# A mixing stage with its phase table from sine and cosine, GpSimd begun sooner, weight splits put ahead of head norms, and the operator products behind the gate

## The chip, the cores and the metric

The kernel runs on one core of one Trainium2 chip. The metric is the device time of one execution in microseconds (us). The profile describes one execution, whose own time stands beside it in the table below.

## The reference

Two blocks follow each other on a sequence of 256 tokens with 1024 channels, all in float32. The first block has two layers, and each layer has a mixing stage and a feed-forward stage:

```
proj = rms_norm(h) @ w_in
u_ssm, u_g, v_g, q, k, v = split(proj)
y_ssm  = s5_mixer(u_ssm, ...)
y_sgu  = spatial_gating(u_g, v_g, ...)
y_diff = diff_attention(q, k, v, ...)
h = h + concat([y_ssm, y_sgu, y_diff]) @ w_out
h = h + conv_gated_mlp(rms_norm(h))
```

The S5 mixer is a diagonal complex recurrence: `a_bar = exp(lam * dt)`, `states[n] = a_bar * states[n-1] + b_bar @ u[n]`, `y = real(c @ states) + d * u`, followed by a GELU and a gate. The differential attention normalises the query and key heads, rotates them, and takes the difference of two softmaxes. The second block is one layer with three attention branches; the change does not touch it.

## The kernel before

Each engine has a block of its own (`@block.sync` for SP, `@block.tensor`, ACT's, GpSimd's, which the profile calls POOL, and VectorE's), in which its instructions stand in the order in which they are issued. Semaphores join the engines. Nothing is scheduled by a planner: the written order is the order.

**Weights.** All weights stream in pairs of 512 KB in the order of `STREAM`. SP loads pair p into one of 7 slots (`LOADS`) of `raw`. ScalarE copies it, rounded, to `whi` (`hi_upto`, L1057; 6 slots, `HIGHS`). VectorE writes the rest, `raw - whi`, to `wlo` (`lo_upto`, L1612). TensorE then adds three products for each pair (L546 to L548 where a token tile is taken alone, L583 to L585 for 256 wide chunks, L590 to L592 otherwise). Once a pair is used, `pair_used` frees its slots. `hi_upto(n)` and `lo_upto(n)` are called at chosen places of the two engines' orders; this sets which split stands ahead of which other work. In layer 0 pairs 0 to 3 are the queries, 4 to 7 the keys, 8 and 9 the S5 input (`ssm_u`), 10 to 13 the gMLP, 14 to 17 the values, 18 to 25 the output projection.

**The mixing stage.** The chunks go through two pairs of PSUM banks in turn (`A` and `B` in the code), and `emptied` makes a chunk wait until the previous user of its banks has been read (`EMPTIED`: for the keys' bank, the rotary products `k_terms` and the squares `hsq_ready`). For queries and keys ScalarE squares the heads (`head_squares`), VectorE sums them (`head_sums`, L1738), GpSimd takes the inverse roots (`head_powers`), VectorE rotates (`rotary`, L1727 to L1732). The gMLP waits for the keys' bank.

**The S5 part** works in chunks of 4 tokens. From the decay parameters (L1669 to L1688, small VectorE operations) GpSimd makes powers of `a_bar` (`amplitude_powers`), multiplies them into the input matrix (`input_powers`, L409 to L412) and the output matrix (`output_powers`, L397 to L399). TensorE projects the inputs (`input_products`, L682); VectorE turns them by a phase table `etab` (`rotate`), scans them, and turns them back. The table has a cosine and a sine for each of 8 states and 64 chunks in every partition, 512 of each. `phase_factors` builds it by repeated squaring and `phase_table` by products (L337 to L356), for layer 0 on VectorE, for layer 1 on GpSimd within the feed-forward stage of layer 0. TensorE makes the operator inside a chunk (`toeplitz_products`, L656 and L658, in two halves) from the input and output powers, and ScalarE copies it out to `mT` (`toeplitz_evac`).

**The attention** goes in three batches: `scores(i)` on TensorE, `batch_max(i)` on VectorE, `exps(i)` on ScalarE (L1183), `combine(i)` on VectorE, `prob_transposes(i)` on TensorE (L764).

The rest of the layer's own work, `output_products` (L697), the gate of the S5 part and the output projection, follows. In layer 1 the powers, the table and the operator are made ahead, in the feed-forward stage of layer 0.

## Time and profile before

| what | value |
|---|---|
| median of 3 runs | 1115.82 us (1114.29 to 1118.82) |
| the profiled execution's own time | 1114.15 us |
| its span, first to last instruction | 1112.2 us |
| TensorE busy | 1021.3 us, 92% |
| VectorE busy | 705.1 us, 63% |
| ScalarE busy | 533.0 us, 48% |
| GpSimd busy | 271.8 us, 24% |
| mean granted TensorE clock | 0.966 |

The busy shares are means over the whole span. The mixing stage of layer 0 lies in the first 170 us, that of layer 1 from about 395 us to 495 us; the feed-forward stages and the second block fill the rest. Times in the rows further below are counted from the span's start.

### The profile page before, as it was taken

How to read it: one execution, taken by the hardware profiler on the slowest of the kernel's cores; microseconds unless marked ns; L12 is line 12 of the kernel's file. 1: busy time of each engine (PE TensorE's matmuls, PEld its weight loads, DVE VectorE, ACT ScalarE, POOL GpSimd, SP SyncE). 2: the span in 40 equal slices, each digit the busy share in tenths (PEclk: the TensorE clock that was granted, in tenths of full speed). 3: DMA queues.
4: the chain of work that ended last, by engine and by line, in shares of the span. 5: the costliest groups of instructions: out<-in, count | busy, mean ns of one | idle time of the engine just before them, and what ended most of it. 6: DMA issues, size and time to landing. Idle time of an engine off the chain costs nothing.

```text
span 1112.2 us, 15875 instructions
## 1 busy us (share of the span) xinstructions
PE 1021.3 (92%) x6060; PEld 888.4 (80%) x6064; DVE 705.1 (63%) x1139; ACT 533.0 (48%) x886; POOL 271.8 (24%) x262
## 2 busy tenths in 40 slices
PE   5577688999999988888999999999999999999997
PEld 4466576999998867677999988887777788888876
DVE  4887635678875465746677775366656655545594
ACT  5224344455664343555566654454344454445532
POOL 1486010098971011010244410002112200000030
PEclk9888689999999999998999999999999999999999
DMA  6332105465546543324655565565544445643452
GB/s 253 128 98 90 39 20 170 154 188 180 173 160 188 163 162 112 114 76 134 213 177 189 185 182 183 185 193 171 164 132 133 141 135 181 163 137 122 135 170 76
DMA packets 48474, 165.96 MB, mean 149 GB/s; under 512 B 6544, under 2 KB 7056, under 8 KB 48400
## 3 DMA queue, kind: packets, MB, share of 16 engines
q1 hardware_dynamic: 48400, 164.95, 46.8%
q8 instruction: 49, 0.80, 0.3%
q14 instruction: 25, 0.20, 0.0%
HBM read 162.83 MB, written 1.05 MB: 147 GB/s over the span
## 4 chain that ended last, share of the span: by engine, by line
PE 82%; DVE 11%; ACT 3%; issue 2%; POOL 1%; DMA 1%; POOLq 0%; DVEq 0%; SPq 0%; ACTq 0%
PE PJ L590 13%; PE PJ L592 13%; PE PJ L591 13%; PE PJ L583 9%; PE PJ L584 9%; PE PJ L585 9%; DVE wlo L1612 2%; PE PJ L546 2%; PE PJ L548 2%; PE PJ L547 2%; PE T L988 1%; PE S L913 1%; PE S L968 1%; PE T L933 1%; PE T L979 1%
## 5 line engine op out<-in xcount | busy, mean ns | idle before, releaser
L1612 DVE TENSOR_TENSOR wlo<-raw,whi 128x1024 fp32r<-128x1024 f32 x294 | 375.5, 1309 | 150.4 <-ACT whi L1057 149.9
L1057 ACT ACTIVATE whi<-raw 128x1024 fp32r<-128x1024 f32 x294 | 302.1, 1062 | 60.2 <-DMA raw<-weights_in 57.4
L583 PE MATMUL PJ<-xth,whi 128*128 128x256 f32 x768 | 221.3, 288 | 10.7 <-DVE wlo L1612 9.1
L590 PE MATMUL PJ<-whi,xth 128*128 128x512 f32 (+1 forms) x480 | 197.0, 411 | 33.7 <-DVE wlo L1612 25.6
L584 PE MATMUL PJ<-xtl,whi 128*128 128x256 f32 x768 | 220.4, 287 | 0.0
L585 PE MATMUL PJ<-xth,wlo 128*128 128x256 f32 x768 | 220.3, 287 | 0.0
L592 PE MATMUL PJ<-whi,xtl 128*128 128x512 f32 (+1 forms) x480 | 189.3, 394 | 0.0
L591 PE MATMUL PJ<-wlo,xth 128*128 128x512 f32 (+1 forms) x480 | 189.0, 394 | 0.0
L583 PEld LDWEIGHTS PJ<-xth,whi 128*128 128x128 f32 x768 | 150.9, 196 | 11.9 <-issue 11.8
L584 PEld LDWEIGHTS PJ<-xtl,whi 128*128 128x128 f32 x768 | 150.8, 196 | 0.1
L585 PEld LDWEIGHTS PJ<-xth,wlo 128*128 128x128 f32 x768 | 150.6, 196 | 0.0
L590 PEld LDWEIGHTS PJ<-whi,xth 128*128 128x128 f32 x480 | 92.5, 193 | 55.0 <-issue 26.3
L1533 POOL TENSOR_TENSOR gtd<-acc 128x512 f32<-128x512 f32 x22 | 79.1, 3597 | 133.0 <-ACT acc L1258 126.4
L1915 DVE SCALAR_TENSOR_TENSOR acc<-PJ,colv,acc 128x255 f32<-128x255 f32 (+1 forms) x176 | 72.5, 475 | 57.5 <-ACT acc L1253 56.7
L592 PEld LDWEIGHTS PJ<-whi,xtl 128*128 128x128 f32 x480 | 92.3, 192 | 20.2
L591 PEld LDWEIGHTS PJ<-wlo,xth 128*128 128x128 f32 x480 | 92.9, 193 | 16.8
L1253 ACT ACTIVATE acc<-PJ,colv 128x256 f32<-128x256 f32 x88 | 42.5, 564 | 97.0 <-PE PJ L585 97.0
L590 PE MATMUL PJ<-whi,hth 128*128 128x512 f32 x144 | 57.0, 396 | 0.0
L591 PE MATMUL PJ<-wlo,hth 128*128 128x512 f32 x144 | 56.9, 395 | 0.0
L592 PE MATMUL PJ<-whi,htl 128*128 128x512 f32 x144 | 56.9, 395 | 0.0
L1591 POOL TENSOR_TENSOR merged<-merged,gt 128x512 f32<-128x512 f32 x6 | 10.6, 1786 | 178.7 <-DVE gt L2108 178.7
L1372 ACT ACTIVATE sm<-S,sx 128x256 f32<-128x256 f32 x24 | 11.4, 474 | 56.6 <-DVE sx L2046 56.6
(394 smaller groups left out, 1467.7 us busy)
## 6 DMA issues: line engine op xcount, KB each, us to landing
raw<-weights_in SPq DMA_DIRECT2D x294, 512.0 KB, 3.5
rt<-bmerge_in SPq DMA_DIRECT2D x6, 256.0 KB, 3.9
xres<-x_in SPq DMA_DIRECT2D x2, 512.0 KB, 5.0
xn<-mem_in SPq DMA_DIRECT2D x2, 512.0 KB, 4.8
y_out<-xn SPq DMA_DIRECT2D x4, 256.0 KB, 2.4
rowv<-rows_in SPq DMA_DIRECT2D x1, 576.0 KB, 9.8
ptmp<-bexp_in SPq DMA_DIRECT2D x2, 256.0 KB, 6.5
cex<-cexp_in SPq DMA_DIRECT2D x2, 256.0 KB, 8.0
```

The costliest lines, as they stand in the source:

```text
L546: pe.matmul(o, h, wh, start=(j == 0 and kk == 0), stop=False, skip_group_check=True)
L583: pe.matmul(o, a, xh[:, k, :], start=(first and f % 2 == 0), stop=False, skip_group_check=True)
L584: pe.matmul(o, a, xl[:, k, :], start=False, stop=False, skip_group_check=True)
L585: m = pe.matmul(o, b, xh[:, k, :], start=False, stop=last, skip_group_check=True)
L590: pe.matmul(o, h, wh, start=first, stop=False, skip_group_check=True)
L591: pe.matmul(o, h, wl, start=False, stop=False, skip_group_check=True)
L592: m = pe.matmul(o, lw, wh, start=False, stop=last, skip_group_check=True)
L1057: act.activation(whi[:, p % HIGHS, :], raw[:, p % LOADS, :], ACT.Copy).then_inc(hi_ready, 1)
L1253: act.activation(acc[:, j % 2, i, :], PJ[BUF[c]][:, i // 2, (i % 2) * TOK:(i % 2 + 1) * TOK], ACT.Identity, scale=colv[:, k + 2:k + 3], bi ...
L1533: pool.tensor_tensor(gtd[:, j % 2, :, :], acc[:, j % 2, 0:2, :], acc[:, j % 2, 2:4, :], ALU.mult).then_inc(sem("gated"), 1)
L1612: dve.tensor_tensor(wlo[:, p % LOADS, :], raw[:, p % LOADS, :], whi[:, p % HIGHS, :].bitcast(F32), ALU.subtract).then_inc(lo_ready, 1)
L1915: dve.scalar_tensor_tensor(out=acc[:, j % 2, i, sh:TOK], in0=PJ[BUF[c]][:, i // 2, (i % 2) * TOK:(i % 2 + 1) * TOK - sh], scalar=colv[:, k ...
```

## The change

- **Phase table.** The factors and products are gone. VectorE computes the phase in turns: seven small operations, one of them a scan that writes the chunk numbers 0 to 63 (`turns`), and three of 512 columns (`phase_turns`), which take off the whole turns. ScalarE then makes the table in four operations of 512 columns (`phase_tables`: two sines, a square, and a scaled copy). For layer 0 these stand on ScalarE between the copies of pairs 11 and 12, ahead of the keys' squares; for layer 1, VectorE's part stands at the ninth unit of the feed-forward stage and ScalarE's behind the last unit's GELU.
- **GpSimd.** The exponential and the two sines of the decay parameters move ahead of the first `norm_hi` on ScalarE, and the four VectorE operations that give the first power move ahead of the norm of token tile 1. The input matrix is loaded and transposed earlier. Both `input_powers` follow each other, both `output_powers` stand ahead of `gate_power`, and the copies of the input matrix (`replicate_inputs`, layer 0) and the mask's casts move to ScalarE.
- **Splits.** `hi_upto` and `lo_upto` are called further ahead around the head squares, sums and rotations, in both layers.
- **TensorE's order, layer 0.** The transposes of token tile 1 stand after the third query pair instead of the fourth. The input matrix's transposes stand between the key pairs. `toeplitz_products` moves from behind `scores(2)` to ahead of `scores(0)`, behind the four gMLP pairs. `input_products` stands ahead of gMLP pairs 2 and 3, in both layers.
- **DMA.** Token tile 1 is asked for after pair 1 instead of pair 0, the input matrix after pair 1 (was 2), the constants after pair 4 (was 3), the output matrix after pair 5 (was 4).

The core of the diff:

```
@@ phase table
-        def phase_factors(eng, link, l, tt_):
...
-        def phase_table(eng, link, k, tmp):
...
+        def phase_turns(dve, link, l):
+            f, k = phase_scratch(l)
+            by_state = f.rearrange("p (s c) -> p s c", s=ST)
+            link(dve.tensor_tensor(by_state, wide(sp_[:, 19, 8 * l:8 * l + 8], NC, 2), wide(chunks[:, :], ST), ALU.mult))
+            link(dve.tensor_scalar(k, f, MAGIC, None, ALU.add))
+            dve.scalar_tensor_tensor(out=f, in0=k, scalar=-MAGIC, in1=f, op0=ALU.add, op1=ALU.subtract).then_inc(sem("turns_ready"), 1)
+        def phase_tables(act, l):
...
+            act.wait_ge(sem("turns_ready"), l + 1)
...
+            act.activation(k, f, ACT.Sin, scale=-3.1415925).then_inc(sem("etab_ready"), 1)
+            act.activation(si, f, ACT.Sin, scale=-6.283185).then_inc(sem("etab_ready"), 1)
+            act.wait_ge(sem("etab_ready"), 4 * l + 1)
+            act.activation(k, k, ACT.Square, scale=math.sqrt(2.0)).then_inc(sem("etab_ready"), 1)
+            act.wait_ge(sem("etab_ready"), 4 * l + 3)
+            act.activation(co, k, ACT.Identity, scale=-1.0, bias=1.0).then_inc(sem("etab_ready"), 1)
@@ TensorE
-                tile_pairs(f"q{l}", 0, 0, range(4), xth, xtl, ready=32 * l)
-                norm_transposes(2 * l, (1,))
+                for j in range(4):
+                    tile_pairs(f"q{l}", 0, j, range(4), xth, xtl, ready=32 * l, upto=j + 1)
+                    if l == 0 and j == 1:
+                        b_transposes(0, B[:, 0, :])
+                    if j == (2 if l == 0 else 3):
+                        norm_transposes(2 * l, (1,))
...
+                pe.wait_ge(sem("bt_ready"), 4 * (l + 1))
                 head_transposes(0, (T0, T1))
...
                 project(f"gmlp{l}", pairs=[1])
+                head_transposes(1, (S0, S1))
+                input_products()
+                project(f"gmlp{l}", pairs=[2, 3])
                 if l == 0:
+                    for b in range(2):
+                        toeplitz_products(0, b, A[:, b, :])
                     pe.wait_ge(sem("maskb_ready"), 3)
                 scores(0)
...
                 scores(2)
-                if l == 0:
-                    for b in range(2):
-                        pe.wait_ge(sem("da_pt"), 1)
-                        if b:
-                            pe.wait_ge(sem("mt_ready"), 4)
-                        toeplitz_products(0, b, B[:, 1, :])
@@ ScalarE
-                hi_upto(s0 + 6)
+                hi_upto(s0 + 9)
                 head_squares(0, A)
...
+                        hi_upto(11 + c)
+                    phase_tables(act, 0)
+                hi_upto(s0 + 13)
                 head_squares(1, B)
@@ GpSimd
             input_powers(pool, link, 0, 0, x_tile(0), ptmp)
+            input_powers(pool, link, 0, 1, x_tile(1), ptmp)
             head_powers(0, 0)
-            head_powers(0, 1)
-            input_powers(pool, link, 0, 1, x_tile(1), ptmp)
...
             folded(0)
+            head_powers(0, 1)
             output_powers(pool, link, 0, 0, ptmp)
+            output_powers(pool, link, 0, 1, ptmp)
+            pool.sem_inc(sem("gpow_ready"), 1)
             gate_power(0)
-            output_powers(pool, link, 0, 1, ptmp)
-            replicate_inputs(0)
@@ VectorE
                 head_sums(0)
-                rotary(0, A, "q_terms", "q_rot")
+                lo_upto(s0 + 7)
+                rotary(0, A, "q_terms", "q_rot", s0 + (10 if l else 8))
+                lo_upto(s0 + 10)
                 if l == 0:
-                    phase_factors(dve, link, 0, pow1)
-                lo_upto(s0 + 9)
+                    turns()
+                lo_upto(s0 + 11)
...
+                lo_upto(s0 + 13)
                 head_sums(1)
...
-                lo_upto(s0 + 17)
+                lo_upto(s0 + 20)
                 batch_max(1)
+                lo_upto(s0 + 21)
                 dve.wait_ge(sem("states_ready"), 2 * (l + 1))
                 combine(0)
```

How the written order moves is shown at three places. In these lists a name left of the arrow is written and one right of it read; `wlo` and `whi` are the two parts of a split.

VectorE, layer 0, at the queries' head sums (`hsk`) and rotation. Before:

```order
L1738 TENSOR_REDUCE hsk<-qh 128x16 [waits hsq_ready]
L1727 TENSOR_TENSOR qh<-PJ,ropeq 128x1024
L1728 TENSOR_TENSOR sm<-PJ,ropeq 128x1024
L1731 TENSOR_TENSOR xn<-qh,sm 128x2x8x32 [waits q_terms]
L1732 TENSOR_TENSOR xn<-qh,sm 128x2x8x32
L343 COPY pw<-sp_ 128x8 [waits q_rot]
L344 COPY pw<-sp_ 128x8 [waits dve_chain]
L337 TENSOR_TENSOR pw<-pw 128x16 [waits dve_chain]
```

And now:

```order
L1734 TENSOR_REDUCE hsk<-qh 128x16 [waits hsq_ready,dve_chain]
L1598 TENSOR_TENSOR wlo<-raw,whi 128x1024 [waits hi_ready]
L1722 TENSOR_TENSOR qh<-PJ,ropeq 128x1024
L1723 TENSOR_TENSOR sm<-PJ,ropeq 128x1024
L1598 TENSOR_TENSOR wlo<-raw,whi 128x1024 [waits hi_ready]
L1727 TENSOR_TENSOR xn<-qh,sm 128x2x8x32 [waits q_terms]
L1728 TENSOR_TENSOR xn<-qh,sm 128x2x8x32
L1598 TENSOR_TENSOR wlo<-raw,whi 128x1024 [waits hi_ready,q_rot]
L1598 TENSOR_TENSOR wlo<-raw,whi 128x1024 [waits hi_ready]
L1686 TENSOR_SCALAR sp_<-sp_ 128x16
```

Four splits (of pairs 6 to 9) stand where the first phase factors stood behind the whole rotation; the phase in turns (`sp_`, then `chunks` and `md`) follows them.

ScalarE, layer 0, ahead of the keys' squares (L1133 before, L1117 now). Before:

```order
L1057 ACTIVATE whi<-raw 128x1024 [waits pair_used,raw_landed0]
L1057 ACTIVATE whi<-raw 128x1024 [waits pair_used,raw_landed1]
L1057 ACTIVATE whi<-raw 128x1024 [waits pair_used,raw_landed2]
L1133 ACTIVATE qh<-PJ 128x512 [waits hss_ready,pair_used]
L1133 ACTIVATE qh<-PJ 128x512
```

And now:

```order
L1125 COPY kmT<-bex 128x1024
L1035 ACTIVATE whi<-raw 128x1024 [waits pair_used,raw_landed4]
L351 ACTIVATE md<-md 128x512 [waits turns_ready]
L352 ACTIVATE etab<-md 128x512
L354 ACTIVATE md<-md 128x512 [waits etab_ready]
L356 ACTIVATE etab<-md 128x512 [waits etab_ready]
L1035 ACTIVATE whi<-raw 128x1024 [waits pair_used,raw_landed5]
L1117 ACTIVATE qh<-PJ 128x512 [waits hss_ready,pair_used]
L1117 ACTIVATE qh<-PJ 128x512
```

The four operations of the table wait for VectorE (`turns_ready`), and the copy of pair 12 and the keys' squares stand behind them.

TensorE, layer 0, at the operator products (`gpw` with `vm` and `kmT`). Before:

```order
L746 MATMUL S<-maskb,identb 128x512 [waits da_exp]
L746 MATMUL S<-maskb,identb 128x512
L749 MATMUL S<-kT,qT 128x256 x4
L656 MATMUL PJ<-gpw,vm 128x128 [waits gpow_ready,da_pt]
L656 MATMUL PJ<-gpw,kmT 128x128
```

And now:

```order
L576 MATMUL PJ<-whi,xtl 128x512
L640 MATMUL PJ<-gpw,vm 128x128 [waits gpow_ready]
L640 MATMUL PJ<-gpw,kmT 128x128
L640 MATMUL PJ<-gpw,vm 128x128
L640 MATMUL PJ<-gpw,kmT 128x128
```

They stood behind the third batch of scores; they stand behind the last gMLP product now, with the scores, the values and all else of TensorE behind them.

## Rows read from the trace of the kernel before

**Rows 1.** Waits of TensorE, whole span: line, waited for, us in total, times, longest.

```profile
PE PJ L590 <- DVE wlo L1612: 25.9, 10, 8.4
```

**Rows 2.** Two stretches: length, busy PE PEld DVE ACT POOL, clock, DMA share, GB/s.

```profile
112.00:140.00 28.00, 17.78 (x81) 14.68 (x82) 16.19 (x32) 10.34 (x28) 0.76 (x3) 0.70 0.12 38
250.00:300.00 50.00, 50.00 (x421) 50.00 (x420) 42.48 (x52) 29.33 (x44) 45.06 (x31) 1.00 0.54 175
```

**Rows 3.** Timeline of TensorE, layer 0: start, us, operation [idle before <- released by].

```profile
16.65 0.77 PE L546 MATMUL PJ<-whi,xth 128*128 128x512 f32 x1 [2.10 <-ACT whi L1057]
...
24.74 0.50 PE L546 MATMUL PJ<-whi,xth 128*128 128x512 f32 x1 [1.44 <-DVE xtl L1630]
...
49.17 0.77 PE L590 MATMUL PJ<-whi,xth 128*128 128x512 f32 x1 [8.35 <-DVE wlo L1612]
...
53.58 0.48 PE L591 MATMUL PJ<-wlo,xth 128*128 128x512 f32 x1
...
70.39 0.48 PE L590 MATMUL PJ<-whi,xth 128*128 128x512 f32 x1
...
73.31 1.08 PE L671 MATMUL PJ<-uT,cst 128*32 128x128 f32 x32
...
91.71 3.68 PE L682 MATMUL T<-uc,bT 128*128 128x64 f32 x32
...
122.88 0.60 PE L764 MATMUL PJ<-cst,sm 128*128 128x128 f32 x4
...
127.67 0.49 PE L656 MATMUL PJ<-gpw,vm 128*128 128x128 f32 x2
...
164.60 0.50 PE L590 MATMUL PJ<-whi,xth 128*128 128x512 f32 x1 [2.01 <-DVE xtl L1873]
```

**Rows 4.** Timeline of VectorE, layer 0.

```profile
30.56 0.17 DVE L1688 TENSOR_SCALAR sp_<-sp_ 128x16 f32<-128x16 f32 x1
...
47.80 3.50 DVE L1612 TENSOR_TENSOR wlo<-raw,whi 128x1024 fp32r<-128x1024 f32 x3
...
59.32 1.21 DVE L1727 TENSOR_TENSOR qh<-PJ,ropeq 128x1024 f32<-128x1024 f32 x1
...
66.87 1.34 DVE L353 TENSOR_TENSOR tq<-pow,pw 128x16 f32<-128x16 f32 x1
```

**Rows 5.** Timeline of ScalarE, layer 0.

```profile
25.19 1.28 ACT L1119 ACT_TABLE_LOAD   x1
...
31.96 2.98 ACT L1057 ACTIVATE whi<-raw 128x1024 fp32r<-128x1024 f32 x3
...
150.35 0.60 ACT L1214 ACTIVATE uT<-PJ 128x512 f32<-128x512 f32 x1 [8.02 <-PE PJ L697]
```

**Rows 6.** Timeline of GpSimd, layer 0 and its feed-forward stage (the last row).

```profile
59.78 2.91 POOL L1439 TENSOR_TENSOR hr<-hr,mhalf 128x16 f32<-128x16 f32 x1
...
65.67 2.51 POOL L411 TENSOR_TENSOR ptmp<-bex,apw 128x768 f32<-128x768 f32 x1
...
101.09 1.99 POOL L397 TENSOR_TENSOR gpw<-gpw,apw 128x1024 f32<-128x1024 f32 x1
...
106.14 3.17 POOL L399 TENSOR_TENSOR gpw<-gpw,ptmp 128x1024 f32<-128x1024 f32 x1
...
308.21 5.50 POOL L1533 TENSOR_TENSOR gtd<-acc 128x512 f32<-128x512 f32 x1 [1.64 <-issue]
```

**Rows 7.** The chain that ended last, in order of time, layer 1.

```profile
472.91 2.29 ACT sm L1183 x8
```

**Rows 8.** Timeline of TensorE, layer 1.

```profile
425.83 0.55 PE L583 MATMUL PJ<-xth,whi 128*128 128x256 f32 x1 [4.51 <-DVE wlo L1612]
...
464.67 0.60 PE L764 MATMUL PJ<-cst,sm 128*128 128x128 f32 x4
...
488.69 0.50 PE L590 MATMUL PJ<-whi,xth 128*128 128x512 f32 x1 [2.01 <-DVE xtl L1873]
```

**Rows 9.** The page's busy tenths of GpSimd in 40 equal slices of the span.

```profile
POOL 1486010098971011010244410002112200000030
```

More of the change, by code:

```diff
@@ L361, in phase_table @@
[L361 to L371 removed]
+        MAGIC = 12582912.0
@@ L1718, in _, with rotary @@
                     link(dve.tensor_tensor(ropeq[:, i, :, :], tb_, wide(row(g, 64 * l, 64), TT), ALU.mult))
-                lo_upto(s0 + 6)
+                lo_upto(s0 + (9 if l else 6))
                 def heads8(ap):
                     return ap.rearrange("p t (g d) -> p t g d", g=8)
-                def rotary(i, src_, terms, done):
+                def rotary(i, src_, terms, done, ahead):
                     co, si = heads8(qn[:, :, :]), heads8(sm[:, 0, :, :])
```

227 lines of the change are left out of this document (98 added, 129 removed).

## The prediction, made before the changed kernel ran

> **What bounds the kernel now.** I read the waits of TensorE first. The wait it has most of is for a split: 25.9 us in ten waits, of which the longest is 8.4 [rows 1]. That says which engine is late, not where. The stretches say where: in the feed-forward stage of layer 0 TensorE is busy for 50.00 of 50.00 us at the full clock, with the DMA engines at 0.54, while in 28 us of layer 0's mixing it is busy for 17.78 and the granted clock is 0.70 [rows 2]. So a stage behind the mixing neither hides a gain nor gives one back, and idle time in the mixing costs twice, once as idle and once as a slower clock behind it. Then the timelines. In layer 0 the third key pair begins at 49.17 after 8.35 us without work, the gMLP at 70.39, the probabilities' transposes at 122.88, the second pair of the output projection at 164.60 [rows 3]. The reader is to see that the wait for the split is a queue on VectorE: the 8.35 us end where the rotation (two operations of 1.21 on 1024 columns, two half as long), five microseconds of small phase factors and the splits ahead in that queue end (three splits together 3.50, from 47.80) [rows 4]. GpSimd is busy in the first tenths of the span and again in the feed-forward stage [rows 9]; in layer 0 its last output power ends at 109.31, and the operator products that read it stand at 127.67 [rows 3, 6].
>
> **The change, place by place.** I follow the new order with durations of the old trace. Times are from the span's start.
>
> *Front.* Splits in front of the squares of token tile 1 save 2.10 of the wait for ScalarE at 16.65, with the idle behind it about 2.4. Transposes of tile 1 behind the third pair hide the 1.44 at 24.74 and most of their own length, 2.1 together. The second tile begins at 20.2 in place of 24.74. Against it: on SP's queue the input matrix now goes ahead of pair 2, and token tile 1 with it, while pair 1 is a whole 512 KB sooner; neither the constants nor the output matrix is read before 33, so their later place costs nothing.
>
> *Third key pair, 49.17 to 36.8.* VectorE has splits 4 and 5 done at 26.0. The fifteen operations of the decay parameters that remain stand .21 apart (the last at 30.56 before): 3.2. GpSimd now works beside them, and one such operation took 1.34 beside a GpSimd operation that began at 65.67 and ended at 68.18 [rows 4, 6]; I add 4 for that: 33.2. Rotary tables (as one operation of 1.2), head sums 1.2 and split 6 at 1.2 [rows 4] end at 36.8. The rotation, the phase factors and two other splits are behind it now. That is the largest single move, 12.4.
>
> *gMLP, 70.39 to 57.0.* TensorE takes the key pair at the slow clock (4.4 = 53.58 - 49.17 for ten of its twelve products), the next pair in 2.9 (73.31 - 70.39), the S5 input and two transposes, and is free at 51.4. The gMLP waits for the keys' bank. On VectorE from 36.8: two rotary products 2.4, three splits 3.5, rotation 1.3, so 44.0, with 0.5 of blocking 44.5. Then the new phase in turns. No row shows it: seven small operations at .21 and one scan, three of 512 columns that I put at the 0.6 that half of 1.21 gives [rows 4]: 3.5, and 1 for blocking, 49. ScalarE's four operations of 512 columns have a GELU of the same shape as nearest row, 0.60 [rows 5]: 2.4, so 51.4. The copy of pair 12 is behind them (2.98 for three [rows 5]): 52.4; its split 53.6; head sums 54.8; two products 57.0. For the sine's price I take 0.60 since the shape is the same; below it nothing excludes 0.4 (-0.8), above it the slowest ScalarE row of twice the columns, 1.0 each (+1.6).
>
> *Inputs.* From 57.0: first gMLP pair slow 4.4, shuffle 1.1, second pair 2.9, head transposes 0.9, input products 3.5: 69.8, against 95.4 (91.71 + 3.68). Two pairs more end at 75.6.
>
> *The new wait.* The operator products now stand in TensorE's order ahead of the scores, so all output powers must be done. GpSimd's inverse root of the keys follows VectorE's sums at 54.8 and took 2.91 [rows 6]: 58. The six steps of the output powers took 8.2 for three, from 101.09 to 109.31, so 16.4: 74.4; with the denser splits I take 76. TensorE is there at 75.6. The wait is forecast to be 0.4 us, and behind it stand scores, values and everything else. Eighteen matmuls at .23 a pair [rows 3] in two halves end at 80.4.
>
> *To the first combination.* ScalarE empties the operator in 8 short copies, 1.7 by estimate, then 0.6, a table load of 1.28 [rows 5] and two small exponentials: 84.4. Four small VectorE steps and the batch maximum (two reductions, as one of 1.2) 86.7. Eight exponentials, by four of them with their sums in 2.29 [rows 7] and half as wide, 3.5: 90.2. VectorE's split, gate norm, second rotation 3.6 and the second maximum end at 95.1; four exponentials 2.3, then the copy of pair 20 0.95 and its split 1.15, because the split now stands ahead of `combine(0)` and its copy behind `exps(1)`: 99.5. Combination 1.5: the first transposes at 101, against 122.88. That new wait costs 2.1 of them.
>
> *Rest of layer 0.* Layer 1 has no operator products in this stretch and takes 24.0 (464.67 to 488.69 [rows 8]); with one pair at the slow clock (4.4 in place of 2.9) I take 25.7: the output pair at 126.7 against 164.60. Layer 0 gains **37.9**.
>
> *Layer 1.* The splits in front of the head sums take away the 4.51 of idle at 425.83 [rows 8] and the slow pair behind it, 1.5: **6.0**. Smaller gaps before it pay for the split behind `exps(1)`. The table costs nothing here: VectorE's part waits for GpSimd's copies in a stretch where TensorE is busy for all of its 50 us [rows 2], its cover being splits that are ahead; ScalarE's part needs one table load more, 1.28 + 2.4 = 3.7, in front of the operator's copy. Were that cover gone, it would cost 3.7 once.
>
> Sum 43.9. The profiled execution took 1114.15; 1114.15 - 43.9 = **1070**. It lies 1.7 under the median of the runs shown, inside their spread.
>
> **One rule against this change.** The 1.34 us of an operation that otherwise takes about .2 ended with the GpSimd operation beside it [rows 4, 6], and GpSimd's own first step took 1.99 where its third, beside splits, took 3.17 [rows 6]. The Trainium skill (SBUF — State Buffer, section Who interferes with whom) says that a VectorE instruction with two SBUF inputs and a GpSimd instruction that reads SBUF exclude each other for a whole instruction, whoever issued first. The trace agrees with it so far. It speaks against the change, which puts GpSimd's long operations and VectorE's splits, both of that kind, into the same microseconds.
>
> **Rivals.**
>
> *Starved GpSimd.* Splits come in one after another, and each step of the output powers waits for several. The longest row beside such work is 5.50 [rows 6]. Six of them are 33: done at 91 in place of 76, and TensorE waits 15 more: **1085**. For it: the splits are denser than before. Against it: the steps of the trace took 8.2 for three although splits ran then too. (If the rule of the Trainium skill's page SBUF — State Buffer, Who interferes with whom, decided each meeting against GpSimd, this would be its time.)
>
> *No conflict worth speaking of.* The 4 + 0.5 + 1 that I put for blocking fall away, the six steps take 12 at 1.99 each, and the gate of the gMLP is TensorE's 51.4: the first transposes at 90 in place of 101: **1059**.
>
> *Slower: the operator products hold up everything.* If the output powers end late, TensorE stands in front of scores and values that could have run. From the powers' end to the output pair I have 126.7 - 76 = 50.7 us. Slower than before it is once they end later than 164.60 + 6.0 - 50.7 = 119.9. That needs the keys' sums some 30 late, at 85 in place of 54.8 (they stand on VectorE behind three splits, the last of which follows ScalarE's table, which itself waits for VectorE), and the starved price of 33 besides: at 126 it gives **1120**. Before, the powers ended at 109.31 and TensorE had other work until then; now it has none. Against it: every step of the chain has its row, and the keys' sums are ahead of the old time throughout.
>
> *Nothing gained.* The front gets ahead, but the weights do not come sooner (a slot is free only when its pair is used), or the output stage finds another late input: **1114**. Against it: DMA moves 175 GB/s where TensorE is full and 38 in the idle stretch [rows 2].
>
> **How the numbers follow.** Within 0.5% is about what a measurement of this kernel can tell from no change; here 5.6 us. Chances: forecast 0.60, starved 0.15, no conflict 0.14, slower 0.06, nothing 0.05. Faster by over 0.5%: 0.60 + 0.15 + 0.14 = 0.89; same 0.05; slower 0.06. The range takes in the first three cases, 0.89 of the chance: down to 1059 less 3 for layer 1's smaller gaps, 1056; up to 1085 with 1.6 for the sines and 3 for clock that stays slow as in the 0.70 stretch [rows 2], 1090.
>
> **What the changed profile would show.** Right: the third key pair near 37, the gMLP near 57, the last output power near 76 with TensorE's wait for it under 2, the transposes near 101, the output pair near 127, and the first granted-clock digits higher. In layer 1 no idle of 4.5 at the second S5 pair. Wrong: a wait of over 5 at the first operator product (starved), splits and small VectorE operations of twice their length, a ScalarE wait at the table that holds up pair 12, or a feed-forward stage that is no longer full.

## The result and the profile after

The changed kernel takes 1077.39 us (median of 4 runs, 1075.94 to 1078.21), the kernel before 1117.05 beside it; the ratio is 0.9646 [0.9621, 0.967]. The profiled execution took 1077.34 with a span of 1075.6, so it is 36.8 us shorter than the profiled execution of before. The forecast was 1070, its range 1056 to 1090.

The waits of TensorE over the whole span (line, waited for, us in total, times, longest) now look like this:

```profile
PE PJ L748 <- DVE sm L1771: 13.4, 2, 8.3
PE PJ L574 <- DVE sm L1723: 5.5, 1, 5.5
PE PJ L574 <- DVE wlo L1598: 4.8, 2, 4.5
```

The wait for a split, 25.9 us in ten places before [rows 1], is 4.8 in two. In its place stands a wait that was not there: 13.4 us, in two places, for `sm`, the combination of two softmaxes. The timeline of TensorE says where (start, us, operation, idle before and its releaser):

```profile
38.20 0.77 PE L574 MATMUL PJ<-whi,xth 128*128 128x512 f32 x1 [4.54 <-DVE wlo L1598]
...
58.48 0.80 PE L574 MATMUL PJ<-whi,xth 128*128 128x512 f32 x1 [5.51 <-DVE sm L1723]
...
67.81 3.68 PE L666 MATMUL T<-uc,bT 128*128 128x64 f32 x32
...
76.88 0.38 PE L640 MATMUL PJ<-gpw,vm 128*128 128x128 f32 x2
...
102.47 1.11 PE L748 MATMUL PJ<-cst,sm 128*128 128x128 f32 x4 [8.31 <-DVE sm L1771]
...
110.94 3.74 PE L681 MATMUL PJ<-sw,gpw 128*128 128x63 f32 x32
...
129.27 0.50 PE L574 MATMUL PJ<-whi,xth 128*128 128x512 f32 x1 [2.01 <-DVE xtl L1866]
...
130.40 0.63 PE L575 MATMUL PJ<-wlo,xth 128*128 128x512 f32 x1
...
424.19 1.11 PE L748 MATMUL PJ<-cst,sm 128*128 128x128 f32 x4 [5.09 <-DVE sm L1771]
...
450.62 0.50 PE L574 MATMUL PJ<-whi,xth 128*128 128x512 f32 x1 [2.01 <-DVE xtl L1866]
```

These answer to [rows 3] and [rows 8]. The third key pair begins at 38.20 (was 49.17), the gMLP at 58.48 (70.39), the input products at 67.81 (91.71), the first transposes at 102.47 (122.88), the output pair of layer 0 at 129.27 (164.60) and that of layer 1 at 450.62 (488.69). The operator products begin at 76.88 with no idle time ahead of them. The row at 130.40 is new too: a product of 0.63, at the lower clock, where the output projection of before ran at 0.39:

```profile
164.94 0.39 PE L591 MATMUL PJ<-wlo,xth 128*128 128x512 f32 x1
```

On VectorE and GpSimd (layer 0), the rows that answer to [rows 4] and [rows 6]:

```profile
27.34 1.46 DVE L1665 TENSOR_TENSOR sp_<-colv 128x16 f32<-128x16 f32 x1
...
33.96 0.17 DVE L1678 TENSOR_SCALAR sp_<-sp_ 128x16 f32<-128x16 f32 x1
...
47.44 1.18 DVE L340 TENSOR_TENSOR md<-sp_,chunks 128x512 f32<-128x512 f32 x1
...
68.71 3.91 DVE L1697 TENSOR_SCALAR rowv<-rowv 128x128 f32<-128x128 f32 x2
72.65 2.38 DVE L1699 TENSOR_SCALAR hb<-colv 128x4 f32<-128x4 f32 x1
...
99.64 1.22 DVE L1598 TENSOR_TENSOR wlo<-raw,whi 128x1024 fp32r<-128x1024 f32 x1 [3.31 <-ACT whi L1035]
```

```profile
59.52 2.46 POOL L382 TENSOR_TENSOR gpw<-gpw,apw 128x1024 f32<-128x1024 f32 x1
...
64.44 3.26 POOL L384 TENSOR_TENSOR gpw<-gpw,ptmp 128x1024 f32<-128x1024 f32 x1
...
72.61 2.39 POOL L384 TENSOR_TENSOR gpw<-gpw,ptmp 128x1024 f32<-128x1024 f32 x1
```

Some small operations take 1.46 where their neighbours take 0.17 (GpSimd works beside them); from 36 us to 96 VectorE has hardly a gap; and the gap of 3.31 at 99.64, ahead of the split of pair 20, is where more than half of TensorE's 8.31 at 102.47 comes from (run e1 below). GpSimd's last output power ends at 72.61 + 2.39 = 75.0. On ScalarE the four table operations took 0.6 each:

```profile
50.44 0.63 ACT L351 ACTIVATE md<-md 128x512 f32<-128x512 f32 x1 [3.84 <-DVE md L342]
...
52.14 0.63 ACT L356 ACTIVATE etab<-md 128x512 f32<-128x512 f32 x1
```

**Where the time went, by landmarks of the two traces.** Up to the output pair of layer 0: 164.60 - 129.27 = 35.3 gained. From there to the second query tile of layer 1 (399.66 before, 366.24 after): 1.9 lost. Layer 1 to its output pair (89.0 before, 84.4 after): 4.6 gained. From there to the end (623.5 before, 625.0 after): 1.5 lost. The sum, before rounding, is 36.6, the difference of the spans. Most of the two losses are slow products like that at 130.40, seven at the start of the output projection in either layer: in layer 0 the way from the second output pair to the next wait of the projection (1.40 us, at 175.34 and 141.65) grew from 10.7 to 12.4. These are two executions. Between the medians, 1117.05 and 1077.39, the gain is 39.7: the execution of before that was profiled is 2.9 us faster than its median.

### The profile page after: what moved, and what is told of

It is laid out like the page before. It is cut to its first block, busy times and chain, and to the rows that moved or that the text cites. A ratio compares the mean times of both kernels' runs of the same rounds, so it can differ in the third digit from the quotient of the medians.

```text
span 1075.6 us, 15765 instructions
## 1 busy us (share of the span) xinstructions
PE 1008.4 (94%) x6060; PEld 877.6 (82%) x6064; DVE 696.1 (65%) x1084; ACT 543.4 (51%) x900; POOL 244.1 (23%) x196
## 4 chain that ended last, share of the span: by engine, by line
PE 80%; DVE 12%; ACT 3%; issue 2%; DMA 1%; POOL 1%; SPq 0%; DVEq 0%; POOLq 0%; ACTq 0%
PE PJ L574 13%; PE PJ L576 13%; PE PJ L575 12%; PE PJ L567 9%; PE PJ L568 9%; PE PJ L569 9%; DVE wlo L1598 3%; PE PJ L530 2%; PE PJ L532 2%; PE PJ L531 2%; PE T L966 1%; DMA raw<-weights_in 1%; ACT whi L1035 1%; PE S L891 1%; PE S L946 1%
## 5 line engine op out<-in xcount | busy, mean ns | idle before, releaser
L1598 DVE TENSOR_TENSOR wlo<-raw,whi 128x1024 fp32r<-128x1024 f32 x294 | 371.3, 1292 | 163.4 <-ACT whi L1035 162.8
L1523 POOL TENSOR_TENSOR gtd<-acc 128x512 f32<-128x512 f32 x22 | 81.6, 3707 | 155.7 <-ACT acc L1245 153.1
L575 PEld LDWEIGHTS PJ<-wlo,xth 128*128 128x128 f32 x480 | 92.7, 193 | 16.9
```

The costliest lines, as they stand in the source:

```text
L575: pe.matmul(o, h, wl, start=False, stop=False, skip_group_check=True)
L1523: pool.tensor_tensor(gtd[:, j % 2, :, :], acc[:, j % 2, 0:2, :], acc[:, j % 2, 2:4, :], ALU.mult).then_inc(sem("gated"), 1)
L1598: dve.tensor_tensor(wlo[:, p % LOADS, :], raw[:, p % LOADS, :], whi[:, p % HIGHS, :].bitcast(F32), ALU.subtract).then_inc(lo_ready, 1)
```

## The experiments

Theory A, drawn from the trace after: VectorE's own queue, without a gap from 36 us to 96, bounds layer 0 up to the first combination, so a part is worth what it takes out of that queue or keeps from waiting in it. The rival is the prediction's own chain: every gate on the way passes on what it gains or loses, and GpSimd's output powers are on it. Runs e1 to e4 undo or mend one thing each in the changed kernel. Their times stand against 1077.4. All runs below were measured later, beside a kernel before at 1114.9 to 1118.8; by their ratios to it e1 gains 8.8 us and e2 to e4 cost 17.0, 19.7 and 18.1, so these differences of medians are good to about 1 us. GpSimd's earlier start, the new place of token tile 1's transposes and the DMA order were not undone by themselves.

**Run e1: the split of pair 20 behind the first combination**

```
                 batch_max(1)
-                lo_upto(s0 + 21)
                 dve.wait_ge(sem("states_ready"), 2 * (l + 1))
                 combine(0)
                 lo_upto(s0 + 22)
```

> The changed kernel with one VectorE line moved, in both layers: the split of pair 20 behind combine(0) in place of ahead of it. Theory A (VectorE is the bound from the second query tile to the first combination, and this split's wait of 3.31 us for a copy that stands behind exps(1) is pure loss): combine(0) begins at 96.4 in place of 100.8 in layer 0, the first probability transposes at 98.1 in place of 102.5, TensorE's wait there 8.3 -> 4; layer 1's wait of 5.1 -> about 1; the slow-clock products at the start of the output projection (1.6 in each layer) may go too. In all 8 to 11 us off 1077.4: 1066 to 1069. Rival (ScalarE's exps(1) and the next splits release the same work anyway): at most 2 us off, 1075.

Measured: 1067.7 us (1066.14 to 1068.25), ratio to before 0.9567 [0.9546, 0.9587]. The timeline of TensorE:

```profile
98.02 1.12 PE L748 MATMUL PJ<-cst,sm 128*128 128x128 f32 x4 [3.26 <-DVE sm L1771]
...
124.57 0.50 PE L574 MATMUL PJ<-whi,xth 128*128 128x512 f32 x1 [2.01 <-DVE xtl L1865]
...
414.82 0.66 PE L748 MATMUL PJ<-cst,sm 128*128 128x128 f32 x4 [0.56 <-DVE sm L1771]
...
440.91 0.50 PE L574 MATMUL PJ<-whi,xth 128*128 128x512 f32 x1 [2.01 <-DVE xtl L1865]
```

Theory A holds in its numbers: the transposes at 98.02 (98.1 expected), the wait in layer 0 down from 8.31 to 3.26, that in layer 1 down from 5.09 to 0.56, 9.7 us off in all, 4.7 of it in layer 0 (129.27 - 124.57) and 5.0 in layer 1. One line of VectorE's order, with nothing that needed it so early, had cost the change a quarter of its gain. This version beats both kernels. The slow products at the start of the projection are gone in layer 1 and still there in layer 0.

**Run e2: the operator products back behind the third scores**

```
                 if l == 0:
-                    for b in range(2):
-                        toeplitz_products(0, b, A[:, b, :])
                     pe.wait_ge(sem("maskb_ready"), 3)
                 scores(0)
...
                 scores(2)
+                if l == 0:
+                    for b in range(2):
+                        pe.wait_ge(sem("da_pt"), 1)
+                        if b:
+                            pe.wait_ge(sem("mt_ready"), 4)
+                        toeplitz_products(0, b, B[:, 1, :])
                 output_products()
```

ScalarE's copies out of the products move behind `exps(2)` with them.

> The changed kernel with the operator products, and ScalarE's copies out of them, back behind scores(2) and exps(2), as before the change; the rest as changed. Theory A: VectorE bounds the time to the first transposes, so these stay at 102.5 +-1; behind scores(2) the second half waits for the copies of the first, the copies stand behind exps(2) (end 114.7), so output products begin at about 118 in place of 109: 8 to 12 us slower, 1086 to 1089. Rival (what the move saves behind scores(2) is paid ahead of scores(0), so its place does not matter): 1077 +-2.

Measured: 1093.3 us (1092.7 to 1093.57), 15.9 above the changed kernel. The timeline of TensorE:

```profile
102.33 1.11 PE L748 MATMUL PJ<-cst,sm 128*128 128x128 f32 x4 [6.80 <-DVE sm L1776]
...
116.99 0.77 PE L640 MATMUL PJ<-gpw,vm 128*128 128x128 f32 x2 [5.17 <-issue]
...
125.14 7.03 PE L681 MATMUL PJ<-sw,gpw 128*128 128x63 f32 x32
...
146.51 0.50 PE L574 MATMUL PJ<-whi,xth 128*128 128x512 f32 x1 [2.01 <-DVE xtl L1871]
```

The transposes did stay (102.33), so the operator's place ahead of the scores costs nothing there, as theory A says. Its price behind them was more than expected: the second half of the products begins after 5.17 of idle at 0.63 to 0.77, the slow clock lasts, and the output products take 7.03, where the changed kernel's take 3.74. I had counted the wait and the copies, not the clock behind them.

**Run e3: VectorE's splits back behind the head sums and rotations**

```
-                lo_upto(s0 + (9 if l else 6))
+                lo_upto(s0 + 6)
...
-                lo_upto(s0 + 7)
-                rotary(0, A, "q_terms", "q_rot", s0 + (10 if l else 8))
+                rotary(0, A, "q_terms", "q_rot", s0 + 6)
                 lo_upto(s0 + 10)
...
-                lo_upto(s0 + 11)
...
-                lo_upto(s0 + 13)
                 head_sums(1)
-                rotary(1, B, "k_terms", "k_rot", s0 + 14)
+                rotary(1, B, "k_terms", "k_rot", s0 + 10)
+                lo_upto(s0 + 14)
```

> The changed kernel with VectorE's splits put back behind the head sums and rotations (splits 6 to 9 behind the queries' rotation, 10 to 13 behind the keys'), in both layers; ScalarE's copies stay ahead. Theory A (VectorE's work in layer 0 is the same in sum): third key pair near 42 in place of 38.2, but transposes of layer 0 at 102.5 +-1.5; layer 1, where VectorE has idle time, loses the 4.7 it gained: 1081 to 1083. Rival (what the prediction's chain says, every gate in layer 0 that waits for a split passes its delay on): 3.7 for layer 0 and 4.7 for layer 1, 1086.

Measured: 1096.13 us (1094.82 to 1098.11), 18.7 above the changed kernel: beyond both theories. Timelines of TensorE and of VectorE:

```profile
42.31 0.77 PE L574 MATMUL PJ<-whi,xth 128*128 128x512 f32 x1 [8.76 <-DVE wlo L1598]
...
63.57 0.76 PE L574 MATMUL PJ<-whi,xth 128*128 128x512 f32 x1 [5.66 <-DVE wlo L1598]
...
77.29 6.92 PE L666 MATMUL T<-uc,bT 128*128 128x64 f32 x32
...
116.59 1.11 PE L748 MATMUL PJ<-cst,sm 128*128 128x128 f32 x4 [7.77 <-DVE sm L1771]
...
144.34 0.50 PE L574 MATMUL PJ<-whi,xth 128*128 128x512 f32 x1 [2.01 <-DVE xtl L1864]
```

```profile
60.56 12.01 DVE L1598 TENSOR_TENSOR wlo<-raw,whi 128x1024 fp32r<-128x1024 f32 x4
...
99.89 0.16 DVE L1827 TENSOR_TENSOR nlam<-lamv 128x1 f32<-128x1 f32 x1 [8.43 <-ACT lamv L1160]
```

The third key pair came at 42.31, as both had it. But theory A's premise, that VectorE's work is the same in sum, is false: four splits that now fall beside GpSimd's output powers took 12.01 us, 3.0 each, in place of some 1.2. The gMLP waits 5.66 for the first of them and begins 5.1 late. The keys' scaling stands behind all four, and TensorE waits 2.97 more for it at 75.53. Behind that wait the clock is low: the input products take 6.92, where the changed kernel's take 3.68. The transposes come 14.1 late. VectorE itself is idle for 8.43 ahead of the first batch maximum, so here it is not VectorE's sum that decides: the delay goes on through TensorE and ScalarE, the way of the rival's chain, at a higher price. Layer 0 loses 15.1 (144.34 - 129.27), and layer 1, whose output pair begins at 472.31, loses 6.6. So the order matters twice: what stands ahead of the gate, and what is thereby kept out of the stretch in which GpSimd multiplies.

**Run e4: the old phase table in layer 0**

```
-                    phase_tables(act, 0)
...
-                phase_turns(dve, link, 0)
...
+                    phase_factors(dve, link, 0, pow1)
                     turns()
...
                 rotary(1, B, "k_terms", "k_rot", s0 + 14)
+                if l == 0:
+                    phase_factors(dve, link, 0, pow8)
...
                 lo_upto(s0 + 15)
                 if l == 0:
+                    for k in range(2):
+                        phase_table(dve, link, k, flat(sv[:, 0, :, :]))
                     lambdas()
```

> The changed kernel with layer 0's phase table made as before, by products on VectorE (first factors behind split 9, second factors behind the keys' rotation, the table behind split 14), and no table operations on ScalarE for layer 0; layer 1 and all else as changed. Theory A (VectorE is the bound until the first combination): it took 17.7 us before, 2.9 of the new work goes: transposes 13 to 15 us later, near 116, time 1089 to 1092. Rival (the prediction's chain, in which only what stands ahead of the keys' head sums is on the path, and the rest lies beside the wait for the output powers): 5.4 - 2.9 - 2.4, so 0 to 4 us slower, 1077 to 1081.

Measured: 1094.25 us (1093.77 to 1095.15), 16.9 above. Timelines of TensorE and VectorE (line numbers are this kernel's):

```profile
79.96 1.97 PE L761 MATMUL S<-cst,xn 128*128 128x128 f32 x8 [8.03 <-DVE xn L1854]
...
120.79 1.12 PE L793 MATMUL PJ<-cst,sm 128*128 128x128 f32 x4 [7.76 <-DVE sm L1814]
```

```profile
68.21 2.33 DVE L385 TENSOR_TENSOR pow<-tq 128x8 f32<-128x8 f32 x1
...
104.09 0.16 DVE L1878 TENSOR_TENSOR nlam<-lamv 128x1 f32<-128x1 f32 x1 [7.64 <-ACT lamv L1204]
```

The cost is a little above theory A's (transposes at 120.79, 116 expected), and the way is another. Operations of 8 columns take 2.33 beside GpSimd, the keys' scaling comes late, TensorE waits 8.03 for it, works at the lower clock behind that wait, and the delay goes on through TensorE and ScalarE, for which VectorE then waits 7.64. VectorE's queue decides, but by what it holds up, not by its sum.

**Runs f1 and f2: two bounds at the first batch maximum.** On run e1; f1 moves the steps that make the lambdas, f2 the four small steps that make `nlam` from them. The split that `lo_upto(s0 + 15)` made is made by the next call.

```
 f1
-                lo_upto(s0 + 15)
-                if l == 0:
-                    lambdas()
                 lo_upto(s0 + 17)
...
                     m.then_inc(sem("w_used"), 1)
+                if l == 0:
+                    lambdas()
                 lo_upto(s0 + 18)
 f2
-                if l == 0:
-                    dve.wait_ge(sem("par_a"), 6)
...
                 batch_max(0)
...
+                if l == 0:
+                    dve.wait_ge(sem("par_a"), 6)
...
                 combine(0)
```

> Run e1 with VectorE's lambda steps of layer 0 moved from behind split 14 to behind the first rotation of the S5 inputs, where GpSimd's output powers are over (three of these steps took 6.3 us in place of 0.8 beside them). Theory A (two chains meet at the first batch maximum: VectorE's own queue, there at 85.5, and ScalarE's, whose exponentials of the lambdas end at 85.7): VectorE comes 4 to 5 us sooner and waits, time 1067.7 +-1. Rival (VectorE alone is the bound, so what the GpSimd lock costs it comes off the end): 4 to 5 us off, 1063.

> Run e1 with the four small steps that wait for ScalarE's exponentials of the lambdas moved from ahead of batch_max(0) to ahead of combine(0), which is their only reader. Theory A: VectorE's own queue takes over as the bound at once, the maximum begins at 85.5 in place of 86.6: about 1 us off, 1066.5 to 1067.5. Rival (the wait for ScalarE alone was the bound): the maximum begins at 83.4, behind the scores; 2 to 3 off, 1065.

Measured: 1067.05 us (ratio to before 0.9549 [0.9519, 0.958]) and 1067.0 (0.9545 [0.9515, 0.9576]), both not to be told from run e1 (0.9567). On VectorE in run f1:

```profile
65.14 9.25 DVE L1598 TENSOR_TENSOR wlo<-raw,whi 128x1024 fp32r<-128x1024 f32 x3
...
85.32 0.16 DVE L1828 TENSOR_TENSOR nlam<-lamv 128x1 f32<-128x1 f32 x1 [1.90 <-ACT lamv L1160]
```

It came sooner, and waited 1.90 for ScalarE, where run e1 waited 0.32. In f2 the maximum began at 85.61, 1.0 sooner than in e1. Both as theory A had it, though 1 us cannot be seen in the time; for f2 the rival's 1065 is set aside by the trace alone, since the maximum did not begin at 83.4. The three splits at 65.14 took 9.25: what the lambdas' steps no longer pay beside GpSimd, the splits do.

**Run f3: both moves.**

> Run e1 with both moves. Theory A: with both bounds gone the first maximum begins at 83.5 to 84, behind the scores, but the next split waits for ScalarE's copy of pair 18 (end 86.7): first transposes 1.5 to 2.5 sooner than run e1's 98.0, 1065 to 1066.5. Rival (each bound alone was worth its full size): 5 to 6 off, 1062.

Measured: 1068.03 us (1066.24 to 1069.57), ratio 0.9557 [0.9524, 0.959]: no gain that the time shows. On VectorE:

```profile
84.18 1.42 DVE L1754 TENSOR_REDUCE st_<-S 128x4 f32<-128x512 f32 x2 [0.23 <-PE S L733]
...
87.58 1.23 DVE L1598 TENSOR_TENSOR wlo<-raw,whi 128x1024 fp32r<-128x1024 f32 x1 [1.78 <-ACT whi L1035]
```

The maximum now follows the scores, and the split behind it waits 1.78 for ScalarE's copy, as expected; but TensorE itself came 0.9 later in this execution, and the 1.5 to 2.5 did not come about. The rival's 5 to 6 did not come either.

**Run f4: no output powers**

```
-            output_powers(pool, link, 0, 0, ptmp)
-            output_powers(pool, link, 0, 1, ptmp)
+            for c in range(2):
+                link(pool.memset(gpw[:, c, :, 1:STEP + 1, :], 0.0))
```

> Run f3 without the six products of the output powers in layer 0: GpSimd fills their place with zeros in two memory sets, so it reads nothing from SBUF there and the operator products wait for nothing; part of the computation is left out. Theory A (GpSimd and VectorE shut each other out for whole instructions, but what that costs VectorE between 59 and 75 is hidden behind TensorE's own queue, which ends its gMLP pairs at 77): VectorE's rotation, key scaling and splits there return from 2.45, 2.87 and 3.43 to 0.7, 1.2 and 1.2 us, and the time moves by less than 1.5 us from run f3. Rival (the lock is on the path): 5 to 8 us off run f3.

Measured: 1068.42 us (1064.44 to 1069.22), ratio 0.9553 [0.9521, 0.9584], against f3's 0.9557. On VectorE:

```profile
60.44 0.68 DVE L1728 TENSOR_TENSOR xn<-qh,sm 128x512 f32<-128x512 f32 x1
...
71.88 1.23 DVE L1739 TENSOR_TENSOR qh<-T,etab 128x1024 f32<-128x1024 f32 x1 [4.53 <-PE T L666]
...
83.04 1.42 DVE L1754 TENSOR_REDUCE st_<-S 128x4 f32<-128x512 f32 x2 [2.03 <-PE S L733]
```

The row at 60.44 was 2.45 in run f3. With GpSimd's products gone VectorE gets ahead and then waits, 4.53 for the input products and 2.03 for the scores. The transposes came at 97.07, 1.15 sooner than in f3, as TensorE's scores did. So in this order the meeting of the two engines is hidden behind TensorE's own queue; in the order of e3 it was not. What it would be worth in the kernel of run g4, where ScalarE's copy of pair 18 no longer comes late, was not run.

**Run g1: the phase in turns behind the keys' scaling.** On run f3, `turns()` and `phase_tables` move away from the gMLP's gate:

```
-                if l == 0:
-                    turns()
                 lo_upto(s0 + 11)
...
                    .then_inc(sem("k_scaled"), 1)
+                if l == 0:
+                    turns()
                 lo_upto(s0 + 17)
```

`phase_tables(act, 0)` moves behind the copies of the keys.

> Run f3 with layer 0's phase in turns moved on VectorE from ahead of the keys' head sums to behind the keys' scaling, and its four table operations on ScalarE from ahead of the keys' squares to behind the copies of the keys. Theory A (two queues of the same length bound the stretch to the first batch maximum, TensorE's from the gMLP's gate on and VectorE's own work from 36 on): the gMLP begins near 53.5 in place of 58.5, but VectorE's sum of work is the same and the turns now lie beside GpSimd's output powers: first transposes at 98 +-2, time 1066 to 1070. Rival (the prediction's chain, in which the gMLP's gate passes on whatever it gains): 4 to 5 us off, 1063.

Measured: 1070.7 us (1067.06 to 1070.93), ratio 0.9585 [0.9559, 0.9611]. On TensorE:

```profile
53.28 0.50 PE L574 MATMUL PJ<-whi,xth 128*128 128x512 f32 x1 [0.33 <-DVE sm L1724]
...
98.52 1.11 PE L748 MATMUL PJ<-cst,sm 128*128 128x128 f32 x4 [4.18 <-DVE sm L1772]
```

The gMLP began 5 us sooner and the transposes did not: the same work came back behind the gate, and dearer: beside GpSimd's output powers the turns took 12.1 (61.70 to 73.79) in place of 5.0. Theory A holds in the trace; the time lies 0.7 above its range. What the gate would be worth with the turns gone altogether, the run does not say.

**Run g2: the gate power between the output powers.** On run e1:

```
             output_powers(pool, link, 0, 0, ptmp)
+            gate_power(0)
             output_powers(pool, link, 0, 1, ptmp)
             pool.sem_inc(sem("gpow_ready"), 1)
-            gate_power(0)
```

> Run e1 with GpSimd's gate power of layer 0 back between the two output powers, as before the change. It waits for the gate's squares, which follow the last gMLP pair (78). Theory A (the operator products stand in TensorE's order ahead of all scores, so the last output power is on the path as soon as it ends behind the gMLP): last output power near 86 in place of 75, TensorE waits 8 to 9 at the second half of the operator products, time 1074 to 1077. Rival (the scores were not the bound, VectorE's queue hides the wait): 1068.

Measured: 1079.02 us (1077.86 to 1080.37), 11.3 above run e1. On TensorE:

```profile
86.81 0.80 PE L640 MATMUL PJ<-gpw,vm 128*128 128x128 f32 x2 [9.88 <-POOLq L1502]
```

This is the mechanism of the prediction's slower rival: 11.9 us of delay in GpSimd (last output power at 86.7, in run e1 at 74.8) is 9.88 of waiting and 11.3 of time. The products begin 9.3 later than in run e1, run slow for most of their length (0.63 to 0.80 in place of 0.38), and the transposes begin 12.2 later (110.22). The wait passes on whole, and the slow clock adds to it; the time is 2 above what I expected.

**Run g3: the splits ahead, alone, in the kernel before.** The hunks of e3 in reverse, and ScalarE's copies with them (`hi_upto` at 9, 13 and 15 in place of 6, 10 and 12).

> The kernel before with one part of the change alone: VectorE's splits and ScalarE's copies as far ahead of the head squares, sums and rotations as in the changed kernel, up to the keys, in both layers. Theory A (the parts share one queue on VectorE, so one part alone is worth much less than its undoing cost, 18.7): third key pair near 40 in place of 49.2, gMLP near 60 in place of 70.4, but the old table, the copies on GpSimd and the operator behind scores(2) take most of that back: 1103 to 1110. Rival (the parts add up): 1097 to 1099.

Measured: 1094.66 us (1093.27 to 1096.62), ratio 0.981 [0.9782, 0.9839], so 20.2 below the kernel before. On TensorE:

```profile
61.13 0.79 PE L590 MATMUL PJ<-whi,xth 128*128 128x512 f32 x1 [6.90 <-DVE sm L1728]
...
151.17 0.50 PE L590 MATMUL PJ<-whi,xth 128*128 128x512 f32 x1 [2.00 <-DVE xtl L1876]
...
467.55 0.50 PE L590 MATMUL PJ<-whi,xth 128*128 128x512 f32 x1 [2.00 <-DVE xtl L1876]
```

Theory A's number fell: this part alone is worth 20.2, which lies below the rival's 1097 to 1099 as well and is about what its undoing cost (18.7), so it does add to the rest. I had counted the gate of layer 0 (70.39 - 61.13 = 9.3) and left two things out: layer 0 gains 13.4 (164.60 - 151.17) up to its output pair, and layer 1 7.7 (488.69 - 467.55 - 13.4). The second number says something on the change as well: the splits alone are worth 7.7 in layer 1, where the order around pair 20 is the old one, and the changed kernel as a whole gains 4.6 there. In layer 0 the agreement with e3 (13.4 and 15.1) is in part luck: in e3 the splits fall beside output powers that stand elsewhere in the kernel before. How the rest of the change, about 20 us, divides is not settled: undoing the operator's place costs 15.9 and undoing the table 16.9, more together than there is, so the two overlap; in what way was not tested.

**Run g4: the copy of pair 18 ahead of the operator's copies.** On run f3:

```
+                hi_upto(s0 + 19)
                 if l == 0:
                     for b in range(2):
                         toeplitz_evac(0, b, A[:, b, :])
```

> Run f3 with ScalarE's copy of pair 18 moved ahead of the operator's copies, in both layers, since VectorE waited 1.78 us for it behind the first maximum. Theory A: the split runs at once, first transposes 1 to 1.8 us sooner, 1065 to 1067 (1.5 below run f3 at most). Rival (the operator's copies are the path: 1.0 later for every one of them): no gain, 1068.

Measured: 1064.61 us (1062.32 to 1065.78), ratio 0.9536 [0.9511, 0.9561]. The transposes come 2.4 sooner than in run f3 (98.22), with 0.72 of waiting:

```profile
95.77 0.66 PE L748 MATMUL PJ<-cst,sm 128*128 128x128 f32 x4 [0.72 <-DVE sm L1772]
```

It is the best median of the study, 3.4 below run f3 and 2.3 below it by the ratios, more than the 1.5 expected; the two intervals of the ratio overlap, and the profiled executions are only 0.5 apart (spans 1064.5 and 1064.0), so all that is sure of it is the 2.4 at the transposes.

## Why the prediction was right, and where it was off

**The bound.** That VectorE's queue held up the weights was right, and runs e3 and g3 show it from both sides (18.7 and 20.2 us).

**Front, second query tile 20.2 forecast, 21.59 measured.** Transposes of the input matrix stand ahead of it (0.6 from 17.01), which the sum left out, and those of tile 1 take 0.8 of TensorE (from 19.11), which it took as mostly hidden. It made no difference: TensorE is idle for 4.54 ahead of the third key pair.

**Third key pair, 36.8 forecast, 38.20 measured.** The decay operations took 7.2 from 26.95 to 34.13, against 3.2 + 4 for blocking; the 4 rested on one row, with no count of how many of the fifteen would meet a GpSimd step (three did), so its fit is luck. The last of the fifteen is the row at 33.96. Late were splits 4 and 5, done at 27.0 in place of 26.0, since GpSimd's steps lay beside them as well, which I had not counted.

**gMLP, 57.0 forecast, 58.48 measured.** The delay of 1.4 is the same, passed on. The phase in turns took 5.0 (4.5 forecast) in nine operations, since the small ones are six, scan and all, and not seven and a scan. The table took 2.4 as forecast: the GELU's 0.60 [rows 5] was the right row for the sine. But this gate is not all that decides the end: in run g1, with the turns moved behind it, TensorE is 5 us sooner here and the transposes are not, because VectorE's queue then holds them.

**The new wait, 0.4 forecast, none measured.** The output powers ended at 75.0 (76 forecast) and TensorE came at 76.88. The starved rival did not occur: the longest of the six steps took 3.26 (64.44), not 5.50. Run g2 shows that the wait would have passed on if it had. (The slower rival's own sum was off: keys' sums at 85, 2.91 and 33 make 121, not 126, which by its rule is 1115 and not 1120.)

**First transposes, 101 forecast, 102.47 measured.** The 1.5 is the delay of the gMLP again. The number is right in part by luck. The chain of the forecast goes through TensorE and ScalarE to the first maximum, and ScalarE was done with its exponentials at 85.1; VectorE's queue, which the forecast did not add up there, reached the same place at 85.8 without a gap. Two queues ended within 1 us of each other. Runs e3, e4 and g2 are held by the first (VectorE is idle for 8.43, 7.64 and 18.11 there), run g1 by the second, and in run e1 the two are 0.32 apart. (Of ScalarE's eight copies the 1.7 of the sum pays four: four took 1.74, and the other four run while TensorE makes the second half.)

**The term that was mis-sized.** "That new wait costs 2.1 of them", I wrote of the split of pair 20. By the prediction's own steps it costs 4.4: the second maximum ends at 95.1 and the split at 99.5, and the 2.1 leaves out `exps(1)`, behind which the copy stands. Run e1 takes the wait away and gains 4.45 at the transposes of layer 0 (102.47 - 98.02). The forecast had that whole cost in its sum for layer 0. What it did not see is that the combination, ready at 96.4, had no need to stand behind the split. In layer 1 it let "smaller gaps before it pay" for the same wait. Those gaps, in the kernel before, were 4.7 together:

```profile
412.77 0.47 PE L590 MATMUL PJ<-whi,xth 128*128 128x512 f32 x1 [1.94 <-DVE wlo L1612]
...
460.52 0.76 PE L590 MATMUL PJ<-whi,xth 128*128 128x512 f32 x1 [2.76 <-DVE wlo L1612]
```

The wait cost 5.0 there (run e1). So layer 1 gained 4.6, not 6.0, although its wait of 4.51 did go; about 1 us of the difference is not traced to a row.

**The stages behind.** They passed the gain on, as [rows 2] said, but for 3.4 us: in the profiled execution the projections begin at the lower clock in both layers, where they did not in that of before. That was not in the forecast, and it is not shown to belong to the change (see the last section): run e1 has no slow products in the projection of layer 1 and takes 625.1 from there to the end all the same, because its clock fell in the second block instead, which the change does not touch (0.92 over 20.9 us from 721.10, where the traces of before and after have 1.00 over 19.4 for the same work). The range of the forecast had 3 us for a slow clock, with a stretch of the mixing itself in mind.

**The rule weighed.** The exclusion of VectorE and GpSimd is real. It costs much where it meets the gate (part of the 18.7 of e3), and nothing that can be measured between 59 and 75, where the change put it (f4 against f3; run f1 had already moved the lambda steps out of it, at no gain). The rival that counted on no conflict, 1059, did not occur: the three small operations at 1.43 to 1.46 are such conflicts, and with those between 59 and 75 gone in run f4 TensorE's queue holds at the same time. The GpSimd row of 3.17 at 106.14 that the prediction reads as beside splits lay beside VectorE's scans of the states (104.15 to 110.39 in the kernel before, 6.24 for two); in the changed kernel, where the output powers are over by then, the same two take 2.48 at 83.26. The blocking ahead of the third key pair was not taken away in any run, so its price there stays an estimate.

The sum: of the 43.9 forecast, layer 0 gave 2.6 less, layer 1 1.4 less, and the stretches behind the two mixing stages, slow products for the most part, took 3.4; that is 36.5, and 36.6 was measured between the spans.

## What to carry to other kernels

Where two engines feed the gate of a third in a written order, the order around a gate can be worth more than the work it moves: look for each instruction that waits and for what stands behind it with its operands ready, as `combine(0)` did. Undo one part at a time and add one part at a time; a part that is worth about the same both ways adds to the rest, if the two runs lose and gain at the same places, and parts whose undoing sums to more than the whole overlap. Before taking work off an engine, see which engine comes next at the same gate: with two queues of nearly equal length, mending one of them shows no gain (f1, f2 and f3 here), although g4, behind them, did come 2.4 sooner at the transposes.

## What the runs showed of the hardware

VectorE's operations with two operands in SBUF waited for whole GpSimd instructions. In the changed kernel the three at 27.34, 28.84 and 30.82, of 0.17 elsewhere, ended at 28.80, 30.29 and 32.25, each 0.03 or 0.04 after the GpSimd step beside it (28.77, 30.25 and 32.21). Four splits of about 1.2 us beside GpSimd's steps took 12.01, three took 9.25 (runs e3, f1), and with two memory sets in place of those steps two took 2.35 (run f4). Two products of 128 columns with a constant took 3.91 at 68.71 and one of 4 columns 2.38 at 72.65, though each reads one operand from SBUF; before, beside GpSimd steps of 0.4 and less, the two took 0.63 and the other 0.19, and in run f4, with GpSimd idle there, 0.48 and 0.17. The Trainium skill (SBUF — State Buffer, section Who interferes with whom) says that copies, casts and products with a scalar can enter a mode that takes the shared ports, and are then shut out too; these two rows agree. GpSimd's root of 128x16 (2.94 at 56.61) slowed nothing: beside it the rotary product at 57.22, with one operand in PSUM, took 1.21, and so did the split at 58.35, with both in SBUF. So these rows do not show whether an operand in PSUM makes a difference.

TensorE's clock fell to the lower level some 1.1 us into the output projection of the changed kernel, after 2.01 of idle ahead of it, and the kernel before kept the higher one after an idle time of the same length. The granted clock over the ten us from 129.27 is 0.83, over the ten from 164.60 of before 1.00. It is not shown to be the change that does it. With the same 2.0 us of idle ahead, the other profiled executions have seven or eight such slow products in layer 0 alone (e1, f4), in layer 1 alone (f1, f3), in both (f2, g1, g2, g4) or in neither (e2, e3, e4, g3), and e1, f1, f2 and f3 differ by a few small steps. In run e1 a fall of the same size stands in the second block, from 721.10. What decides it is open.
